# Sums of squares for the norms: one fp32 matmul by ones against two fp32r matmuls of a split sum, in a two-block transformer kernel

## The reference, cut to what matters

```python
def rms_norm(x, g, eps=NORM_EPS):
    x32 = x.astype(jnp.float32)
    y = x32 * lax.rsqrt(jnp.mean(x32 * x32, axis=-1, keepdims=True) + eps)
    return (y * g.astype(jnp.float32)).astype(x.dtype)

        x = x + rms_norm(merged @ w_out[l], norm_mix_post_g[l])
        h = rms_norm(x, norm_ffn_pre_g[l])
        f = (jax.nn.silu(h @ w_gate[l]) * (h @ w_up[l])) @ w_down[l]
        x = x + rms_norm(f, norm_ffn_post_g[l])
```

## Time and profile before

| what | value |
|---|---|
| median of 3 runs | 1955.38 us (1955.15 to 1955.60) |
| span of the profiled execution | 1954.3 us |
| between that span and the median | 1.1 us |
| PE busy | 1933.8 us, 99% of the span |
| PEld, DVE, ACT, POOL busy | 81%, 51%, 39%, 12% |
| chain that ended last | PE 93%, DVE 3%, ACT 2%, DMA 1%, issue 1% |
| granted TensorE clock | 9 (nine tenths or more) in all 40 slices |

### The profile page before, as it was taken

One profiled execution on the slowest core, in us unless ns is written; L12 is line 12 of the kernel. 1 busy time (PEld: TensorE's weight loads), 2 busy tenths in 40 slices (PEclk: granted clock), 3 DMA queues, 4 the chain that ended last, 5 costly groups with the idle time before them and its releaser, 6 DMA issues.

```text
span 1954.3 us, 22926 instructions
## 1 busy us (share of the span) xinstructions
PE 1933.8 (99%) x9122; PEld 1577.5 (81%) x9122; DVE 1005.8 (51%) x1525; ACT 753.3 (39%) x1165; POOL 237.4 (12%) x240
## 2 busy tenths in 40 slices
PE   9999999999999999999999999999999999999998
PEld 7777788878888888788888888888787788888887
DVE  6677545374334335633333467787754443334335
ACT  6344534453222234432322346655643343222224
POOL 5210001201011011010100121222010011011010
PEclk9999999999999999999999999999999999999999
DMA  6222233333333323333333232222232233333313
GB/s 173 58 65 65 66 92 106 115 100 97 97 96 97 97 85 115 90 98 97 97 97 97 79 105 67 64 65 65 87 93 59 80 94 98 96 97 97 97 59 103
DMA packets 340764, 176.25 MB, mean 90 GB/s; under 512 B 6482, under 2 KB 339379, under 8 KB 340659
## 3 DMA queue, kind: packets, MB, share of 16 engines
q1 hardware_dynamic: 340658, 174.79, 30.5%
HBM read 172.67 MB, written 2.10 MB: 89 GB/s over the span
## 4 chain that ended last, share of the span: by engine, by line
PE 93%; DVE 3%; ACT 2%; DMA 1%; issue 1%; SPq 0%; POOL 0%; ACTq 0%; DVEq 0%
PE ps L1101 28%; PE ps L1105 28%; PE ps L1103 28%; PE ps L1161 1%; PE ps L1141 1%; PE ps L1194 1%; PE ps L1150 1%; PE ps L1239 1%; PE ps L1114 1%; PE ps L1257 1%; PE ps L1124 1%; DVE WL L1549 1%; PE ps L1131 0%; PE ps L1175 0%; DMA TS<-in_x 0%
## 5 line engine op out<-in xcount | busy, mean ns | idle before, releaser
L1101 PE MATMUL ps<-HH,WH 128*128 128x512 f32 x1728 | 687.6, 398 | 1.7 <-ACT HH L1310 1.7
L1105 PE MATMUL ps<-HL,WH 128*128 128x512 f32 x1728 | 673.9, 390 | 0.8 <-DVE HL L1570 0.8
L1549 DVE TENSOR_TENSOR WL<-RAW,WH 128x1024 fp32r<-128x1024 f32 (+3 forms) x335 | 400.6, 1198 | 532.0 <-ACT WH L1300 531.8
L1103 PE MATMUL ps<-HH,WL 128*128 128x512 f32 x1728 | 673.2, 390 | 0.8 <-DVE WL L1549 0.8
L1300 ACT ACTIVATE WH<-RAW 128x1024 fp32r<-128x1024 f32 (+3 forms) x335 | 337.6, 1010 | 523.8 <-PE ps L1105 517.4
L1101 PEld LDWEIGHTS ps<-HH,WH 128*128 128x128 f32 x1728 | 324.5, 188 | 77.8 <-issue 9.7
L1103 PEld LDWEIGHTS ps<-HH,WL 128*128 128x128 f32 x1728 | 324.6, 188 | 72.3 <-issue 5.5
L1105 PEld LDWEIGHTS ps<-HL,WH 128*128 128x128 f32 x1728 | 324.3, 188 | 71.8 <-DVE HL L1570 2.1
L1101 PE MATMUL ps<-GH,WH 128*128 128x512 f32 x688 | 269.2, 391 | 0.0
L1105 PE MATMUL ps<-GL,WH 128*128 128x512 f32 x688 | 268.0, 390 | 0.0
L1103 PE MATMUL ps<-GH,WL 128*128 128x512 f32 x688 | 267.8, 389 | 0.0
(11 more groups left out here) (201 smaller groups left out, 1558.3 us busy)
## 6 DMA issues: line engine op xcount, KB each, us to landing
RAW<-in_ffn_w_gu SPq DMA_DIRECT2D x88, 512.0 KB, 3.8
RAW<-in_w_in SPq DMA_DIRECT2D x67, 512.0 KB, 3.9
RAW<-in_ffn_w_down SPq DMA_DIRECT2D x32, 512.0 KB, 4.1
RAW<-in_w_gate SPq DMA_DIRECT2D x22, 512.0 KB, 3.8
RAW<-in_w_up SPq DMA_DIRECT2D x22, 512.0 KB, 3.8
RAW<-in_w_out SPq DMA_DIRECT2D x16, 512.0 KB, 4.2
RAW<-in_mem_w_kv SPq DMA_DIRECT2D x16, 512.0 KB, 4.0
RAW<-in_w_down SPq DMA_DIRECT2D x16, 512.0 KB, 4.1
```

Source lines behind the costliest of these rows:

```text
L1101: e.matmul(bk, wh, xh, start=k == 0, stop=False)
L1103: e.matmul(bk, wl, xh, start=False, stop=False)
L1105: last = e.matmul(bk, wh, xl, start=False, stop=k == kt - 1)
L1549: e.tensor_tensor(at.weight(n, "L"), m["RAW"][:, n % NRAW, 0:kt, :], at.weight(n, "H").bitcast(F32), ALU.subtract).then_inc(*sg.inc("lo", n))
```

## The change

All sums of squares over partitions become two fp32r matmuls by fp32r ones. A new step `halves` splits the sum: ACT writes its rounded half with a Copy into a second tile of the ring (`("hi", acc)`), seen as fp32r (`TR`, the same memory as `TS`), then DVE writes sum minus that half over the sum, as fp32r too. PE multiplies the ones by the first, then by the second, into one bank. `onesD`, `one128` and `blk` are made in spare memory and copied to fp32r by POOL. For streams 1 and 2 POOL first adds the squares of chunks c-1 and c (c odd), so that four sums are split and multiplied instead of eight.

The places of the new step: in the accumulator norms it stands right behind the last addition or the single square. In stream 0 it stands at k step 4 of the third projection. In the memory rows a step of the pipeline later. In streams 1 and 2 the halves of pair c-3 stand behind the feed of chunk c, for c = 3, 5 and 7; those of the last pair behind the weight split at the start of the first gate and up tiles. PE's matmuls for a pair stand ahead of k steps 2, 4 and 6 and behind step 7.

```diff
@@ feed
         if gen in SUMMED:
             self.tiles.take((key, c))
             self.step("square", key, (key, c), ("X", c), T, ("x", (gen, c)))
+            if c % 2:
+                self.step("square_pair", key, c)
+                self.tiles.give((key, c), ("sqp", (key, c - 1)))
+                if c > 2:
+                    self.halves((key, c - 3), ("sqp", (key, c - 3)))
         else:
-            self.square(key, c, ("X", c), T, ("x", (gen, c)))
+            done = self.square(key, c, ("X", c), T, ("x", (gen, c)))
+            if c == KD - 1 and gen:
+                self.halves(key, done)
+
+    def halves(self, acc, ev, cols=T):
+        self.tiles.take(("hi", acc))
+        self.step("halves", acc, ev, cols)
@@ ffn, first gate and up tiles of a summed stream
-                    sums = iter(range(-1, KD))
+                    at = iter(range(KD))
                     def before():
-                        c = next(sums)
-                        if c >= 0:
-                            self.sum_square(("n", gen), c)
+                        k = next(at)
+                        if k == 0:
+                            self.halves((("n", gen), KD - 2), ("sqp", (("n", gen), KD - 2)))
+                        elif k % 2 == 0:
+                            self.sum_square(("n", gen), k - 2)
                     mg, mu = self.mtiles([sg, su], ("H", gen, 0), [bg, bu], before=before)
-                    before()
+                    self.sum_square(("n", gen), KD - 2)
@@ post_norm
+        self.halves(acc, acc_ev)
         made = [self.memory_mtile(cols[0])]
-        self.rstd(("post", gen), acc, acc_ev, "onesD", 0)
+        self.rstd(("post", gen), acc, "onesD", 0)
@@ first_three
         def before():
-            if next(at) == 6:
+            k = next(at)
+            if k == 4:
+                self.halves(("n", 0), ("acc_last", ("n", 0)))
+            if k == 6:
                 self.norm(0)
@@ heads (h; t and g likewise)
-            ev = self.square(("h", u), 0, bank, T, ("vl", (u, 0)))
+            self.halves(("h", u), self.square(("h", u), 0, bank, T, ("vl", (u, 0))))
             yield
-            self.rstd(("h", u), ("h", u), ev, "one128", 1)
+            self.rstd(("h", u), ("h", u), "one128", 1)
@@ tensor_program, rstd (sum_square likewise)
-        g.wait_ge(*sg.at(*ev))
+        g.wait_ge(*sg.at("sh", acc))
         wait_all(at.bank_free(("stat", key)))
-        e.matmul(bk[:, 0:cols], m[ones], at.tile(acc)[:, 0:cols], start=True, stop=True).then_inc(*sg.inc("stat", key))
+        e.matmul(bk, m[ones], at.rounded(("hi", acc))[:, 0:cols], start=True, stop=False)
+        g.wait_ge(*sg.at("sl", acc))
+        e.matmul(bk, m[ones], at.rounded(acc)[:, 0:cols], start=False, stop=True).then_inc(*sg.inc("stat", key))
@@ scalar_program
+    def halves(acc, ev, cols):
+        g.wait_ge(*sg.at(*ev))
+        wait_all(at.tile_free(("hi", acc)))
+        e.activation(at.rounded(("hi", acc))[:, 0:cols], at.tile(acc)[:, 0:cols], ACT.Copy).then_inc(*sg.inc("sh", acc))
@@ vector_program
+    def halves(acc, ev, cols):
+        v = at.tile(acc)[:, 0:cols]
+        g.wait_ge(*sg.at("sh", acc))
+        g.wait_ge(*sg.at(*ev))
+        e.tensor_tensor(at.rounded(acc)[:, 0:cols], v, at.rounded(("hi", acc))[:, 0:cols].bitcast(F32), ALU.subtract).then_inc(
+            *sg.inc("sl", acc))
@@ pool_program
+    def square_pair(key, c):
+        a, s = at.tile((key, c - 1)), at.tile((key, c))
+        g.wait_ge(*sg.at("sq", (key, c)))
+        g.wait_ge(*sg.at("sq", (key, c - 1)))
+        e.tensor_tensor(a, a, s, ALU.add).then_inc(*sg.inc("sqp", (key, c - 1)))
```

More of the change, by code:

```diff
@@ L194, in sum_square, with rstd @@
         self.step("sum_square", key, c)
-        self.tiles.give((key, c), ("ssq", (key, c)) if c < KD - 1 else ("stat", key))
-    def rstd(self, key, acc, ev, ones, eps, cols=T):
+        done = ("ssq", (key, c)) if c < KD - 2 else ("stat", key)
+        self.tiles.give((key, c), done)
+        self.tiles.give(("hi", (key, c)), done)
+    def rstd(self, key, acc, ones, eps, cols=T):
         if acc is not None:
@@ L200, in rstd @@
             self.tiles.give(acc, ("stat", key))
+            self.tiles.give(("hi", acc), ("stat", key))
         self.tiles.take(("R", key))
         self.tiles.take(("Ra", key))
-        self.step("rstd", key, acc, ev, ones, eps, cols)
+        self.step("rstd", key, acc, ones, eps, cols)
         self.banks.give(("stat", key), ("rb", key))
@@ L209, in norm @@
             self.held[gen] = True
-            self.rstd(("n", gen), None if gen in SUMMED else ("n", gen), ("acc_last", ("n", gen)), "onesD", 0)
+            self.rstd(("n", gen), None if gen in SUMMED else ("n", gen), "onesD", 0)
         return ("n", gen)
@@ L578, in memory_in @@
             yield
-        self.rstd("mem", "macc", ev, "onesD", 0, 256)
+        self.halves("macc", ev, 256)
+        yield
+        self.rstd("mem", "macc", "onesD", 0, 256)
         self.step("memory_r")
@@ L731, in stick_unit @@
         self.tiles.give(v[0], mm)
-        ev = self.square(key, 0, bank, T, mm)
+        self.halves(key, self.square(key, 0, bank, T, mm))
         yield
-        self.rstd(key, key, ev, "blk", 0)
+        self.rstd(key, key, "blk", 0)
         self.head_norm(key, bank, mm, COL["sb_gnorm_2"] + u)
@@ L797, in gated_unit @@
         self.tiles.give(v[0], mm)
-        ev = self.square(("g", u), 0, bank, T, mm)
+        self.halves(("g", u), self.square(("g", u), 0, bank, T, mm))
         yield
-        self.rstd(("g", u), ("g", u), ev, "one128", 0)
+        self.rstd(("g", u), ("g", u), "one128", 0)
         yield
@@ L975, in tile, with rounded @@
         return self.mem["TS"][:, self.plan.tiles.slot[key], :]
+    def rounded(self, key):
+        return self.mem["TR"][:, self.plan.tiles.slot[key], :]
     def bank(self, key):
@@ L1480, in store @@
             e.activation(y, y, ACT.Copy, scale=m["ST"][:, h, i:i + 1]).then_inc(*sg.inc("oa", (h, a)))
-    todo = dict(split=split, split_half=split_half, feed_x=feed_x, feed=feed, square=square, rstd=rstd, func=func, plain=plain, turn=turn, split_tile=split_tile,
+    todo = dict(split=split, split_half=split_half, feed_x=feed_x, feed=feed, square=square, halves=halves, rstd=rstd, func=func, plain=plain, turn=turn, split_tile=split_tile,
                 memory_hi=memory_hi, small_terms=small_terms, exps=exps, turn_probs=turn_probs, stick_part=stick_part,
@@ L1577, in square_last, with rstd @@
         e.tensor_tensor(a, a, s, ALU.add).then_inc(*sg.inc("acc_last", acc))
-    def rstd(key, acc, ev, ones, eps, cols):
+    def halves(acc, ev, cols):
[4 more added lines that the diff above has]
+            *sg.inc("sl", acc))
+    def rstd(key, acc, ones, eps, cols):
         bk, R, a = at.bank(("stat", key))[:, 0:cols], at.tile(("R", key))[:, 0:cols], at.tile(("Ra", key))[:, 0:cols]
@@ L2055, in program @@
         mem["X"] = sb("X", [P, KD, T])
-        mem["TS"] = sb("TS", [P, NTILE, T])
+        with nc.sbuf_tensor("TS", [P, NTILE, T], F32) as ts:
+            mem["TS"] = ts
+        mem["TR"] = sb("TR", [P, NTILE, T], F32R)
         mem["LB"] = sb("L", [P, 2, 1280])
```

40 lines of the change are left out of this document (24 added, 16 removed).

## The result

Slower, and by more than forecast: 1975.93 us median of 4 runs (1973.66 to 1976.43) against 1955.49 (4 runs, 1955.15 to 1957.21) of the kernel before on the same chip. The medians lie 20.4 us apart; the ratio over all runs is 1.0098 [1.0086, 1.0109], which is +19 us (16.8 to 21.3). Forecast were +11.5, and at most +15.6. The profiled execution has a span of 1973.7 us, 19.4 more than the one before (1954.3).

A forecast was written before the change was run, and what follows sets the result against it. PE, busy 99%, was taken to bound the kernel. On the span of 1954.3 us, 6.0 + 5.4 + 2.4 + 0.7 - 3.0 = +11.5 gave 1965.8, as median 1966.9; range 1956 to 1971.

The forecast's parts named there:

- What bounds the kernel, what is taken out: Whole kernel: PE, 99% busy, sets the time; two fp32r matmuls instead of one fp32 save 0.40 us per sum.
- Streams 1 and 2, DVE's queue and POOL: Summed streams: DVE's fuller queue makes each 1.4 us longer, POOL's pair additions 4.0 more; with post norms 6.0 and 5.4.
- rival A: Streams 1 and 2: POOL gives way, each pair addition waits for DVE; +3.5 us, 1958.9; chance 0.17.
- Stream 0: Stream 0's norm: rounding and subtraction stand behind weight splits, second matmul ends at 30.5 instead of 28.1; cost 2.4 us.
- The others: Remaining norms, in heads, streams 3 and 5 and memory rows: seven sums gain 0.40 each, memory rows 0.2; 3.0 us gained.
- the third stick-breaking pair: Second block's heads: nothing gained at this pair's sum.
- 0.2 for the memory rows: Memory rows' norm: its 256-column sum by two fp32r matmuls gains 0.2 us.
- Rival C: Second block's heads cost 0.6 us in each of six, the 3.0 gain is lost; +18.1, 1973.5; chance 0.11.
- Rival B: Streams 1 and 2: PE paces them, so 5.0 us is gained twice; -9.9 in all, 1945.5; chance 0.07.

The follow-up runs named there:

- sums_fp32: The changed kernel, but the sums over eight chunks in streams 1 and 2 by eight fp32 matmuls as before, no POOL pairs or halves there: 1964.24 us.
- sums_fill: The changed kernel with 25 more fp32r matmuls in each of streams 1 and 2, where PE waits anyway: 1975.80 us.
- s0_fill: The changed kernel with 12 more fp32r matmuls on PE in stream 0 ahead of the norm's sum, where PE waits anyway: 1973.82 us.
- s0_fp32: The changed kernel, but stream 0's norm by one fp32 matmul as before, without halves there: 1969.11 us.
- heads2_fp32: The changed kernel, but the eight norms of the second block's gated and stick-breaking heads by one fp32 matmul each, no halves: 1973.84 us.
- mem_fp32: The changed kernel, but the memory rows' norm by one fp32 matmul and without the extra step between its last addition and its sum: 1973.28 us.
- sums_late: The changed kernel, but in streams 1 and 2 all four sums behind PE's last k step and the last halves ahead of DVE's weight split: 1973.68 us.
- s0_early: The changed kernel, but stream 0's rounding and subtraction queued right behind the last addition, ahead of the two weight splits: 1971.48 us.
- pairs_only: The changed kernel, but in streams 1 and 2 POOL's four pair sums go to PE by fp32 matmuls, without Copies and subtractions: 1967.00 us.

## Why the prediction was wrong, step by step

- **What bounds the kernel, what is taken out** (0.40 for a sum). Right. Each sum that PE paces gave 0.39 to 0.45.
- **Streams 1 and 2, DVE's queue and POOL.** Right, in mechanism and in size: 11.4 forecast, 11.6 measured, 10.9 of it given back by sums_fp32, which leaves the post norms' halves where they are (0.8 in stream 1). The price of 1.1 per pair is shown (1.03 to 1.13). The Trainium skill's rule (SBUF — State Buffer, Who interferes with whom), that a whole instruction excludes the other and issue order decides, agrees with the rows of these two streams; rival A, the other case of the same rule, didn't occur in them (no pair above 1.59).
- **Stream 0: "The second matmul ends its turn at 30.5 ... Cost 2.4".** This step failed. The wait itself came out near the forecast (2.9 us in sums_fill, where no fall followed) and its consequence was missing: after 3.5 us with one matmul in them PE ran at half its clock for twelve matmuls. s0_fill shows that 2.6 of the 5.7 us are this, s0_fp32 that all of it hangs on this norm. The trace of before shows the lower level nowhere but in its last microseconds, and, at 58 to 60 us, a wait of 1.8 us without a fall; I let PE wait longer and priced only the length. The Trainium skill states this (TensorE: Matmul & The Clock Gate, HAM oscillation — how this bites in real kernels): matmuls that follow a long enough wait of PE start cold. The trace agrees, 0.43 and 0.23, but sums_fill shows the same wait with no fall behind it.
- **"The others": the third stick-breaking pair, "nothing gained".** Too good by 3.1 us over the heads. Copy and subtraction push the ACT and DVE chain, the scans among it, 1.3 later (the first scan starts 19.7 after its place before, 1391.80 and 1372.10, where PE entered this block, at 1222, 18.4 later), while PE's 0.4 gains let it come earlier: its wait grew by 2.2, and the fall of the clock added 0.9 net of what a later wait took up. I had counted each sum's 0.4 as final; heads2_fp32 shows that those ahead of a wait for DVE are only lent.
- **"The others": "0.2 for the memory rows".** The saving was there and 1.8 was lost behind it. I had looked for POOL's port only where the change adds POOL work; it also decides anew who goes first where POOL and DVE already met. That this is the collision of the earlier trace rows, and that the loss hangs on the memory norm's form, is shown. Why it is now DVE that waits stays open: both engines' operations start in the same order and at the same distance as before, so the starts recorded do not tell which goes first, and mem_fp32 undoes sum and extra step together.
- **The chances.** Rival C was closest by the time it gave (1973.5), but by its mechanism only in part: the cost in the heads was one place with a clock fall, not 0.6 in each of six. Rival B is excluded by the rows of streams 1 and 2 (+11.6 where it had -10.0), and by sums_late: with PE's order free it is up to 6.1 us ahead and has 0.8 of it at the end. The range's upper end left out that several small terms could all err upward: 3.3, 1.8 and 3.1 are 8.2 us, of which start and end take back 0.3; the rest is the 7.9 us by which the profiled execution missed the forecast.

## What to carry to other kernels

When work moves from a saturated PE to engines whose queues are full in just those stretches, price the queue that ends the stretch, not PE: 17 us less of PE work became some 20 us more time. An elementwise addition on an idle POOL is no gift to DVE; here it cost DVE 1.1 us against 0.6 for doing it itself. And where a forecast makes PE wait, add what the clock does after the wait, if PE's own work bounds what follows.

## What the runs showed that I had not expected

The same wait can be followed by a fall or not. At 58 to 60 us (in the time of the kernel before) all these kernels have PE idle for 1.8 us ahead of the differential scores. The kernel before, and s0_early, from 62 to 64:

```profile
62.00:64.00 2.00, 2.00 (x10) 1.64 (x9) 2.00 (x9) 0.00 (x0) 1.83 (x2) 1.00 0.28 83
```

```profile
62.00:64.00 2.00, 2.00 (x6) 1.47 (x5) 2.00 (x5) 0.00 (x0) 1.56 (x2) 0.57 0.85 248
```

With the fall that place is 1.6 us longer; it fell there in seven of the twelve kernels' profiled executions, and not in the changed kernel's. In stream 0 the fall's length differs too: 12 slow matmuls in the changed kernel, and in four others with the same wait (sums_fp32, sums_late, mem_fp32, pairs_only) 6 or 7 of them, a fall that costs 1.2 to 1.3 us less; in sums_fill there is none. This may be part of the spread, which was not traced run by run: runs of the changed kernel lie between 1973.66 and 1976.43 with mean clocks of 0.994 and 0.990. What decides it was not tried. In the three places where s0_fill and sums_fill put work into PE's idle time, it did not fall.
